# Two pairs of FFN chunks as seven block products each, in a float32 decoder trunk

## The chip, the cores and the metric

One core of a Trainium2 chip runs the whole program. Times are microseconds of device time for one execution; lower is better. The engines are TensorE (PE, with its weight loads as PEld), VectorE (DVE), ScalarE (ACT), GpSimd (POOL) and SyncE (SP), which issues the large loads. Each runs its own instructions in program order and waits on semaphores.

## The reference

The input is x, 256 tokens of 1024 float32 values. Two layers follow, each an FFN, a token mixer and a second FFN, with a norm ahead of each:

```
def rms_norm(x, g):
    y = xf * lax.rsqrt(jnp.mean(xf * xf, axis=-1, keepdims=True) + EPS)
    return y * g
def swiglu(h, w_in, w_out):
    a, b = jnp.split(h @ w_in, 2, axis=-1)
    return (jax.nn.silu(a) * b) @ w_out
...
x = x + 0.5 * swiglu(rms_norm(x, norm_g[l, 0]), ffn_w_in[l, 0], ffn_w_out[l, 0])
x = x + mixer(rms_norm(x, norm_g[l, 1]))
x = x + 0.5 * swiglu(rms_norm(x, norm_g[l, 2]), ffn_w_in[l, 1], ffn_w_out[l, 1])
```

w_in is 1024 x 5632 (2816 columns of a, 2816 of b), w_out is 2816 x 1024. The mixer of layer 0 is a sparse attention over compressed, selected and window keys (NSA), that of layer 1 an attention with forget gates (Fox) on keys and values projected once (KV). The order of stages is FFN 0, NSA, FFN 1, KV, FFN 2, Fox, FFN 3.

## The kernel before

**Numbers in two parts.** A float32 product is made of three matmuls of rounded parts: hi x hi, hi x lo and lo x hi (`three`). hi is a cast to float32r, lo is what the cast leaves. So each weight value is cast on ScalarE and subtracted on VectorE before TensorE uses it.

**Units.** Weights come in units of 128 x 2048 values (1 MB in two transfers). SyncE loads unit u into `raw`, ScalarE casts it to `whi` (`hi`), VectorE writes `wlo` (`lo`), TensorE uses it in 24 matmuls of 128 x 512 (two token tiles x four row blocks x three). Each of the three buffers has three places, and unit u takes place u % 3: the load of u waits for the split of u - 3, the cast of u for TensorE's use of u - 3 (`s_used`).

**An FFN.** The 2816 hidden columns are 11 chunks of 256 (j = 0 to 10). A chunk has two input units a and b, the upper and the lower half of the 1024 rows, each with 256 columns of a and 256 of b; their product stands in the banks `inb[0]` and `inb[1]`, one per token tile. ScalarE takes silu of the a columns (`silu_tile`), VectorE multiplies (`hidden_tile`), four transposes turn the result into `tb[0]` (`hidden_turn`), ScalarE and VectorE split it into `ghi` and `glo`. The chunk's output unit o is 256 rows of w_out; it adds into the four banks `acc`. TensorE's order is a1 b1 o0, a2 b2 o1, and so on: a chunk's output is multiplied one chunk later. Chunks 1 to 9 run in loops (`Fori`) on every engine; the last chunk takes one token tile after the other, so that its hidden part is ready in time. Then the next stage's first unit begins.

**Other work.** GpSimd makes the table of relative biases in FFN 0, adds attention results in NSA, and makes the decay terms at the start of FFN 2. The reciprocal roots of the norm, `rstd`, are applied per token after the matmuls, so TensorE can start before they are known.

Lines: `three` is L403 to L405, turns L512 and L397, `hi` L922 and L935 (loop), `lo` L1312 and L1329 (loop), silu L988, hidden product L1376, its split L997 and L1385, decay terms L1877 to L1881, the adds of the residual L1426 and L1436.

Of the kernel before, what the change touches and what calls it, by code (L numbers as in the profile page):

```python
# [70 lines left out]

TURNS = ["ffn0", "nsa", "ffn1", "kv", "ffn2", "fox", "ffn3"]
# [29 lines left out]
def yoco_trunk(nc, x, norm_g, ffn_w_in, ffn_w_out, nsa_w_in, nsa_cmp_pos, nsa_cmp_w1, nsa_cmp_w2,  # L102
               nsa_w_out, rel_bias, kv_norm_g, fox_w_kvf, fox_b_f, fox_w_q, fox_w_out, final_g, out):
    ctx = ExitStack()
    with ctx:
# [27 lines left out]
        fhi = sb("fhi", [P, 16, GN], F32R)  # L133
        flo = sb("flo", [P, 16, GN], F32R)
# [51 lines left out]
        win_hi = fhi[:, :, :].rearrange("p t n -> p (t n)")  # L186
        win_lo = flo[:, :, :].rearrange("p t n -> p (t n)")
# [3 lines left out]
        ghi_last = fhi[:, :, :].rearrange("p t n -> p (t n)")[:, 0:2 * SEQ].rearrange("p (k n) -> p k n", k=2)  # L191
        glo_last = flo[:, :, :].rearrange("p t n -> p (t n)")[:, 0:2 * SEQ].rearrange("p (k n) -> p k n", k=2)
        gwhi = ghi[:, :, :].rearrange("p a n -> p (a n)")
        gwlo = glo[:, :, :].rearrange("p a n -> p (a n)")
# [4 lines left out]
        finalb = work[:, 0:D]  # L199
# [36 lines left out]
        s_silu = sem("silu_done")  # L236
        s_g = sem("hidden_ready")
# [74 lines left out]
        def _(sp):  # L312
            def load(u, halves, number=None):


                if number is not None or u >= RING:
                    sp.wait_ge(s_lo, (u if number is None else number) - RING + 1)
                for dst, src in halves:
                    sp.dma_start(dst, src).then_inc(s_raw[u % RING], 16)

            def ffn_in(f, j, half, u):
                w = ffn_w_in[f // 2, f % 2][half * 512:(half + 1) * 512, :]
                w = w.rearrange("(k p) n -> p k n", p=P)
                r = raw[u % RING][:, :].rearrange("p (k n) -> p k n", k=4)
                return [(r[:, :, 0:FC], w[:, :, bass.ds(j * FC, FC)]),
                        (r[:, :, FC:2 * FC], w[:, :, bass.ds(j * FC + DFF, FC)])]

            def ffn_out(f, j, u):
                w = ffn_w_out[f // 2, f % 2]
                r = raw[u % RING][:, :].rearrange("p (k n) -> p k n", k=2)  # L330
                return [(r[:, k, :], w[bass.ds(j * FC + k * P, P), :]) for k in range(2)]

            def ffn(f):
                b = U_FFN[f]
                for i in range(2):
                    if f or i:
                        load(b + i, ffn_in(f, 0, i, b + i))
                        continue
                    (ra, wa), (rb, wb) = ffn_in(0, 0, 0, 0)
                    for k, arrived in ((0, s_first), (2, s_raw[0])):  # L340
                        for r, w in ((ra, wa), (rb, wb)):
                            sp.dma_start(r[:, k:k + 2], w[:, k:k + 2]).then_inc(arrived, 16)
                    sp.dma_start(xs[:, 1, :], x[0, P:2 * P, :]).then_inc(s_x[1], 16)
                with sp.Fori(1, NJ) as j:
                    for i in range(3):
                        u = b + 2 + i
                        halves = ffn_in(f, j, i, u) if i < 2 else ffn_out(f, j - 1, u)

                        load(u, halves, 3 * (j - 1) + max(u, RING))
                u = b + FFN_UNITS - 1  # L350
                load(u, ffn_out(f, NJ - 1, u))

            def matrix(w, b, chunks):

                for c, col in enumerate(chunks):
                    for i in range(2):
                        u = b + 2 * c + i
                        wr = w[i * 512:(i + 1) * 512, col:col + CW].rearrange("(k p) n -> p k n", p=P)
                        r = raw[u % RING][:, :].rearrange("p (k n) -> p k n", k=4)
                        load(u, [(r[:, 0:2], wr[:, 0:2]), (r[:, 2:4], wr[:, 2:4])])  # L360
# [4 lines left out]
            for xk in range(2):  # L365
                for i in range(2):
                    u = U_CMP[xk] + i
                    wr = nsa_cmp_w1[0, xk, i * 1024:(i + 1) * 1024, :].rearrange("(k p) n -> p k n", p=P)
                    r = raw[u % RING][:, :].rearrange("p (k n) -> p k n", k=8)
# [18 lines left out]
        def _(pe):  # L388
# [94 lines left out]
            def out_part(slot, t, k, first=False):  # L483

                for n in range(2):
                    mm = out_columns(slot, t, k, n, first=first)
                return mm

            def out_columns(slot, t, k, n, last=False, first=False):
                h_hi, h_lo = (ghi_last, glo_last) if last else (ghi, glo)  # L490
                tok = slice(t * P, (t + 1) * P)
                col = slice(k * D + n * CW, k * D + (n + 1) * CW)
                return three(acc[2 * t + n][:, :], h_hi[:, k, tok], h_lo[:, k, tok],
                             whi[slot][:, col], wlo[slot][:, col], first and k == 0, last and k == 1)

            def out_last(slot, t):

                for n in range(2):
                    out_columns(slot, t, 0, n, True)
                    mm = out_columns(slot, t, 1, n, True)  # L500
                    mm.then_inc(s_used if (t, n) == (1, 1) else s_out_bank, 1)
# [6 lines left out]
            def hidden_turn(need, tiles=range(NT)):  # L508
                pe.wait_ge(s_g, need)
                for k in range(2):  # L510
                    for t in tiles:
# [3 lines left out]

            def ffn(f, following=None):

                b, n0, h0 = U_FFN[f], NJ * f, (NJ + 1) * f
# [5 lines left out]

                unit_in((b + 2) % RING, 0, inb, b + 3)
                hidden_turn(2 * (n0 + 1))
                unit_in((b + 3) % RING, 1, inb, b + 4)
                pe.wait_ge(s_lo, b + 5)
                pe.wait_ge(s_glo, 1 + h0)
                slot = (b + 4) % RING  # L530
                out_part(slot, 0, 0, True)
                out_part(slot, 0, 1)
                out_part(slot, 1, 0, True)
                hidden_turn(2 * (n0 + 2))
                out_part(slot, 1, 1).then_inc(s_used, 1)

                with pe.Fori(2, NJ - 1) as j:
                    for half in range(2):
                        u = b + 2 + half
                        unit_in(u % RING, half, inb, 3 * (j - 1) + u + 1)  # L540
                    pe.wait_ge(s_lo, 3 * (j - 1) + b + 5)
                    pe.wait_ge(s_glo, j + h0)
                    slot = (b + 4) % RING
                    out_part(slot, 0, 0)
                    out_part(slot, 0, 1)
                    out_part(slot, 1, 0)
                    hidden_turn(2 * j + 2 * n0 + 2)
                    out_part(slot, 1, 1).then_inc(s_used, 1)

                u = b + 3 * (NJ - 1) - 1  # L550
                for t in range(NT):
                    for half in range(2):
                        pe.wait_ge(s_lo, u + half + 1)
# [1351 lines left out]
```

## Time and profile before

| | us |
|---|---|
| median of 3 runs | 1053.43 (1053.39 to 1054.06) |
| profiled execution | 1053.35 |
| its span, first to last instruction | 1051.4 |
| TensorE busy | 1040.1 (99%) |
| VectorE busy | 598.2 (57%) |
| ScalarE busy | 525.5 (50%) |
| GpSimd busy | 73.4 (7%) |
| mean granted TensorE clock | 0.995 of full speed |

The profile is of one execution. A span leaves out about 2 us that the measured time has. Start times are microseconds from the first instruction. Matmul records overlap: the distance from start to start, not the duration, is what one costs. The four FFN stages lie at about 0 to 192, 356 to 550, 602 to 788 and 856 to 1046 us.

### The profile page before, as it was taken

The page shows a single profiled execution, that of the slowest core. Times are in us where ns is not written, and L with a number is a line of the kernel's source. Part 1 is how long each engine was busy: PE and PEld are TensorE (multiplying, and loading weights), DVE is VectorE, ACT ScalarE, POOL GpSimd, SP SyncE. Part 2 cuts the span into 40 slices and gives each one's busy share as a digit, 9 for nine tenths or more (in the row PEclk, how much of TensorE's full clock was granted, in tenths as well). Part 3 has the DMA queues.
Part 4 walks back from the last instruction along what each step waited for, and adds up shares of the span by engine and source line. Part 5 has one row for each costly group of instructions (what it writes and reads, how often), then busy time and mean ns, then how long its engine had stood idle before and what let it go on. Part 6 is the DMA issues. An engine that isn't in the chain of part 4 may idle for free.

```text
span 1051.4 us, 14153 instructions
## 1 busy us (share of the span) xinstructions
PE 1040.1 (99%) x5156; PEld 865.4 (82%) x5156; DVE 598.2 (57%) x833; ACT 525.5 (50%) x692; POOL 73.4 (7%) x108
## 2 busy tenths in 40 slices
PE   9999999999999999999999999999999999999997
PEld 7888888888888888888888888888888888888886
DVE  5554454677576564455467765544566656445544
ACT  7434434657475554434456554344356655443443
POOL 0041000000013000000000291000000000000000
PEclk9999999999899999999999999999999999999999
DMA  7686757457401366555545665555446146655541
GB/s 243 239 214 208 218 187 249 145 175 225 136 2 41 120 202 198 191 168 199 183 150 188 221 204 193 184 198 190 170 160 200 42 140 201 199 183 177 199 160 41
DMA packets 128709, 182.45 MB, mean 174 GB/s; under 512 B 5960, under 2 KB 100272, under 8 KB 128544
## 3 DMA queue, kind: packets, MB, share of 16 engines
q1 hardware_dynamic: 127040, 176.18, 50.5%
q0 software_dynamic: 1456, 5.72, 2.4%
q8 instruction: 24, 0.39, 0.2%
q14 instruction: 13, 0.11, 0.0%
q10 hardware_dynamic: 176, 0.05, 0.0%
HBM read 180.34 MB, written 1.59 MB: 173 GB/s over the span
## 4 chain that ended last, share of the span: by engine, by line
PE 97%; DVE 2%; ACT 1%; issue 0%; POOL 0%; POOLq 0%; DVEq 0%; ACTq 0%
PE inb L403 16%; PE inb L405 16%; PE inb L404 16%; PE acc L403 13%; PE acc L405 13%; PE acc L404 13%; PE acc L613 2%; PE tb L512 2%; PE tb L625 2%; PE inb L640 2%; PE inb L637 1%; PE tb L592 1%; PE tb L397 1%; PE acc L397 0%; DVE tlo L1346 0%; PE inb L824 0%
## 5 line engine op out<-in xcount | busy, mean ns | idle before, releaser
L1329 DVE TENSOR_TENSOR wlo<-raw,whi 128x2048 fp32r<-128x2048 f32 x108 | 250.0, 2315 | 233.6 <-ACT whi L935 233.6
L935 ACT CAST whi<-raw 128x2048 fp32r<-128x2048 f32 x108 | 206.5, 1912 | 217.5 <-PE acc L405 117.8
L403 PE MATMUL inb<-whi,thi 128*128 128x512 f32 x720 | 281.7, 391 | 0.0
L405 PE MATMUL inb<-whi,tlo 128*128 128x512 f32 x720 | 280.5, 390 | 0.0
L404 PE MATMUL inb<-wlo,thi 128*128 128x512 f32 x720 | 280.2, 389 | 0.0
L405 PEld LDWEIGHTS inb<-whi,tlo 128*128 128x128 f32 x720 | 135.1, 188 | 28.4
L404 PEld LDWEIGHTS inb<-wlo,thi 128*128 128x128 f32 x720 | 135.2, 188 | 28.0
L403 PEld LDWEIGHTS inb<-whi,thi 128*128 128x128 f32 x720 | 135.2, 188 | 28.0
L1312 DVE TENSOR_TENSOR wlo<-raw,whi 128x2048 fp32r<-128x2048 f32 x55 | 129.1, 2352 | 43.8 <-ACT whi L922 43.5
L403 PE MATMUL acc<-whi,ghi 128*128 128x512 f32 x320 | 128.5, 402 | 0.0
L405 PE MATMUL acc<-whi,glo 128*128 128x512 f32 x320 | 125.1, 391 | 0.0
L404 PE MATMUL acc<-wlo,ghi 128*128 128x512 f32 x320 | 124.6, 389 | 0.0
L922 ACT CAST whi<-raw 128x2048 fp32r<-128x2048 f32 x55 | 105.2, 1918 | 11.7 <-PE acc L405 9.5
L988 ACT ACTIVATE sa<-inb,rstd 128x256 f32<-128x256 f32 x80 | 34.0, 471 | 137.8 <-PE inb L405 137.8
L403 PE MATMUL acc<-whi,thi 128*128 128x512 f32 x224 | 89.4, 399 | 1.3 <-DVE tlo L1346 0.6
L405 PE MATMUL acc<-whi,tlo 128*128 128x512 f32 x224 | 87.6, 391 | 0.0
L404 PE MATMUL acc<-wlo,thi 128*128 128x512 f32 x224 | 87.3, 390 | 0.0
L405 PEld LDWEIGHTS acc<-whi,glo 128*128 128x128 f32 x320 | 60.0, 188 | 12.9
L1376 DVE SCALAR_TENSOR_TENSOR gg<-inb,rstd,sa 128x256 f32<-128x256 f32 x80 | 35.4, 479 | 61.6 <-ACT sa L988 61.6
L404 PEld LDWEIGHTS acc<-wlo,ghi 128*128 128x128 f32 x320 | 60.3, 188 | 11.1
L403 PEld LDWEIGHTS acc<-whi,ghi 128*128 128x128 f32 x320 | 60.1, 188 | 11.0
L403 PEld LDWEIGHTS acc<-whi,thi 128*128 128x128 f32 x224 | 42.1, 188 | 11.5 <-issue 1.2
(231 smaller groups left out, 980.1 us busy)
## 6 DMA issues: line engine op xcount, KB each, us to landing
raw<-in_ffn_w_in SPq DMA_DIRECT2D x174, 512.0 KB, 4.7
raw<-in_ffn_w_out SPq DMA_DIRECT2D x88, 512.0 KB, 4.0
raw<-in_nsa_w_in SPq DMA_DIRECT2D x20, 512.0 KB, 4.1
raw<-in_fox_w_kvf SPq DMA_DIRECT2D x16, 512.0 KB, 4.3
raw<-in_nsa_cmp_w SPq DMA_DIRECT2D x8, 512.0 KB, 4.8
raw<-in_nsa_w_out SPq DMA_DIRECT2D x8, 512.0 KB, 4.5
raw<-in_fox_w_q SPq DMA_DIRECT2D x8, 512.0 KB, 4.5
raw<-in_fox_w_out SPq DMA_DIRECT2D x8, 512.0 KB, 4.6
```

The costliest lines, as they stand in the source:

```text
L403: pe.matmul(o, lh, rh, start=start, stop=False, skip_group_check=True)
L404: pe.matmul(o, lh, rl, start=False, stop=False, skip_group_check=True)
L405: return pe.matmul(o, ll, rh, start=False, stop=stop, skip_group_check=True)
L512: mm = pe.transpose(tb[0][:, k * SEQ + t * P:k * SEQ + (t + 1) * P], gg[:, t, k * P:(k + 1) * P], ident[:, :])
L613: mm = pe.matmul(acc[2 * (n % 2) + h][:, c0:c0 + keys], qT[rows, p, t * P:(t + 1) * P], kT[rows, kidx, 0:keys], start=True, stop=True)
L625: mm = pe.transpose(tb[h][:, i * P:(i + 1) * P], probs[:, n % 2, c:c + P], ident[:, :])
L922: act.copy(whi[u % RING][:, :], raw[u % RING][:, :]).then_inc(s_hi, 1)
L935: act.copy(whi[u % RING][:, :], raw[u % RING][:, :]).then_inc(s_hi, 1)
L988: act.activation(sa[:, t, :], banks[t][:, 0:FC], ACT.Silu, scale=rstd[:, t:t + 1]).then_inc(s_silu, 1)
L1312: dve.tensor_tensor(wlo[u % RING][:, :], raw[u % RING][:, :], whi[u % RING][:, :].bitcast(F32), ALU.subtract).then_inc(s_lo, 1)
L1329: dve.tensor_tensor(wlo[u % RING][:, :], raw[u % RING][:, :], whi[u % RING][:, :].bitcast(F32), ALU.subtract).then_inc(s_lo, 1)
L1376: dve.scalar_tensor_tensor(out=gg[:, t, :], in0=banks[t][:, FC:2 * FC], scalar=rstd[:, t:t + 1], in1=sa[:, t, :], op0=ALU.mult, op1=ALU.mu ...
```

## The change

Chunks 3 and 4, and 7 and 8, become a pair. `KINDS = "nnnsnnsnn"` lists the segments of an FFN: n a single chunk, s a pair. For a pair the input side is the product of the tokens (256 x 1024, four blocks A11 to A22 of 128 x 512) with weights (1024 rows x 512 columns of a and 512 of b, four blocks B11 to B22 of 512 x 512). It is made from seven block products in place of eight, each 12 matmuls:

- on the tokens: S1 = A21 + A22, S3 = A11 - A21, S2 = S1 - A11, S4 = A12 - S2, made by GpSimd once per FFN, then split by ScalarE and VectorE;
- on the weights: T1 = B12 - B11, T3 = B22 - B12, T2 = B11 + T3, T4 = B21 - T2 (as the code forms them), by VectorE once per pair;
- products M1 (A11, B11), M5 (S1, T1), M2 (A12, B21), M6 (S2, T2), M3 (S4, B22), M7 (S3, T3), M4 (A22, T4), combined by VectorE and ScalarE into the four results u3, c12, c22, c21. M2 adds to M1's bank, M3 to M5's, M7 to M6's.

The four weight blocks of a pair are loaded into `nat`, `xn` and `work`, outside the three load buffers, one behind each of four unit loads. A pair's TensorE order is M1 M5 o M2 M6 (o) M3 M7 M4, the first turn, then the next chunk's a, in which the second turn follows. M4 goes into `tb[1]`. The token sums need the tokens times `rstd` in a row layout: two matmuls (`rstd_rows`) turn `rstd` into rows. GpSimd's bias and decay work waits for later units. All loops over chunks are written out, and the last chunk is treated as the others, with two output units at the end. `qT` now lies in `nat`, the final gain in `vx`.

```
+KINDS = "nnnsnnsnn"
+LOADS_AT_ONCE = 1
...
+def ffn_order():
+    order = []
+    for kind, j, rows in SEGMENTS:
+        if kind == "n":
+            order += [("a", j), ("b", j)] + [("o", r) for r in rows]
+        else:
+            order += [("M1", j), ("M5", j), ("o", rows[0]), ("M2", j), ("M6", j)]
+            order += [("o", r) for r in rows[1:]] + [("M3", j), ("M7", j), ("M4", j)]
+    return order + [("o", r) for r in LAST_ROWS]
...
+            def pair_weights(f, n, i):                       # SyncE
+                b, j = U_FFN[f], PAIRS[n]
...
+                elif i == 0:
+                    u = b + UNIT_OF["M7", PAIRS[n - 1]]
+                    sp.wait_ge(s_tw, 4 * (len(PAIRS) * f + n))
+                    sp.wait_ge(s_lo, u + 1)
...
+                    if n < len(PAIRS) and (kind, j) == (("o", 0) if n == 0 else ("b", PAIRS[n - 1] + 2)):
+                        i = 0
+                    if i is not None and kind in "abo":
+                        for i in range(i, i + LOADS_AT_ONCE):
+                            pair_weights(f, n, i)
...
+            def ffn_pair(f, j, rows):                        # TensorE
+                n = len(PAIRS) * f + PAIRS.index(j) + 1
+                product(f, j, "M1", "A11", inb[1], True, False)
...
+                product(f, j, "M5", "S1", tb[1], True, False)
+                out_rows(f, rows[0])
+                pe.wait_ge(s_m1, n)
+                product(f, j, "M2", "A12", inb[1], False, True)
+                product(f, j, "M6", "S2", inb[0], True, False)
+                for r in rows[1:]:
+                    out_rows(f, r)
+                pe.wait_ge(s_m5, n)
+                product(f, j, "M3", "S4", tb[1], False, True)
+                pe.wait_ge(s_u2, n)
+                product(f, j, "M7", "S3", inb[0], False, True)
+                pe.wait_ge(s_c12, n)
+                product(f, j, "M4", "A22", tb[1], True, True)
+                pair_turn(f, j, 0)
...
+            def ffn_chunk(f, j, rows):                       # ScalarE
+                if kind == "s":
+                    pair_hidden_hi(f, before, 1)
...
+                if SEGMENTS[i + 1:i + 2] and SEGMENTS[i + 1][1] == PAIRS[0]:
+                    for name in SPLITS:
+                        tokens_hi(f, name)
+                hi(a + 3)
...
+            def ffn_chunk(f, j, rows):                       # VectorE
+                if pair == PAIRS[0]:
+                    for name in SPLITS:
+                        tokens_lo(f, name)
+                if pair:
+                    t1_weights(f, pair)
+                lo(a + 3)
...
+                for t in range(NT):
+                    hidden_tile(2 * (NSEG * f + i) + t, t)
+                if pair:
+                    t3_weights(f, pair)
+                lo(a + 4)
+                for r in rows:
+                    u = b + UNIT_OF["o", r]
+                    chunk_hidden_lo(f, j)
+                    if u + 3 < b + FFN_UNITS:
+                        lo(u + 3)
+                if pair:
+                    t2_weights(f, pair)
+            def ffn_pair(f, j, rows):                        # VectorE
+                lo(m["M1"] + 3)
+                t4_weights(f, j)
+                lo(m["M5"] + 3)
+                lo(m["M5"] + 4)
+                lo(m["M2"] + 3)
...
+                dve.tensor_tensor(c12, inb[0][:, :], u3, ALU.add).then_inc(s_u2, 1)
+                lo(m["M6"] + 3)
+                for r in rows[1:]:
+                    lo(m["M6"] + 4)
...
+                dve.tensor_tensor(c12, tb[1][:, :], c12, ALU.add).then_inc(s_c12, 1)
...
+                dve.tensor_tensor(c12, c12, sa_p, ALU.mult).then_inc(s_g, 1)
+                lo(m["M3"] + 3)
...
+                dve.tensor_tensor(u3, inb[0][:, :], u3, ALU.add).then_inc(s_u3, 1)
...
+                dve.tensor_tensor(c22, c22, u3, ALU.add).then_inc(s_c22, 1)
+                lo(m["M7"] + 3)
+                pair_hidden_lo(f, j, 0)
...
+                dve.tensor_tensor(c22, c22, sa_p, ALU.mult).then_inc(s_g, 1)
+                lo(m["M4"] + 3)
...
+            def token_sums(f):                               # GpSimd
+                pool.wait_ge(s_lo, U_FFN[f] + 2)
...
+                pool.wait_ge(s_rc, f + 1)
...
+                pool.tensor_tensor(four(c22), a21, a22, ALU.add).then_inc(s_as, 1)
+                pool.tensor_tensor(a21, a11, a21, ALU.subtract).then_inc(s_as, 1)
+                pool.tensor_tensor(a11, four(c22), a11, ALU.subtract).then_inc(s_as, 1)
+                pool.tensor_tensor(a12, a12, a11, ALU.subtract).then_inc(s_as, 1)
...
+            token_sums(2)
+            pool.wait_ge(s_used, U_FFN[2] + UNIT_OF["b", PAIRS[-1] + 2] + 1)
```

## Rows read from the trace of the kernel before

**Rows 1.** The page: busy time of the engines, and the chain that ended last.

```profile
PE 1040.1 (99%) x5156; PEld 865.4 (82%) x5156; DVE 598.2 (57%) x833; ACT 525.5 (50%) x692; POOL 73.4 (7%) x108
...
PE 97%; DVE 2%; ACT 1%; issue 0%; POOL 0%; POOLq 0%; DVEq 0%; ACTq 0%
```

**Rows 2.** Windows, FFN 1: busy us (instructions) by engine, clock, DMA share, GB/s.

```profile
356.00:550.00 194.00, 194.00 (x894) 160.71 (x893) 104.16 (x99) 91.32 (x103) 0.00 (x0) 1.00 0.55 180
```

**Rows 3.** Timeline, TensorE, FFN 1: start, us, engine, line, operation.

```profile
405.39 0.39 PE L403 MATMUL inb<-whi,thi 128*128 128x512 f32 x1
...
410.84 0.39 PE L403 MATMUL inb<-whi,thi 128*128 128x512 f32 x1
```

**Rows 4.** Timeline, ScalarE, FFN 1, one chunk; idle time before in brackets.

```profile
399.69 0.84 ACT L988 ACTIVATE sa<-inb,rstd 128x256 f32<-128x256 f32 x2 [3.53 <-PE inb L405]
...
405.59 1.91 ACT L935 CAST whi<-raw 128x2048 fp32r<-128x2048 f32 x1 [3.26 <-PE acc L405]
...
416.48 0.84 ACT L988 ACTIVATE sa<-inb,rstd 128x256 f32<-128x256 f32 x2 [3.53 <-PE inb L405]
```

**Rows 5.** Groups of instructions, whole span: count, busy us, mean ns, idle before.

```profile
L1385 DVE TENSOR_TENSOR glo<-tb,ghi 128x512 fp32r<-128x512 f32 x40 | 27.3, 683 | 0.0
...
L997 ACT CAST ghi<-tb 128x512 fp32r<-128x512 f32 x40 | 23.2, 579 | 6.0 <-PE tb L512 6.0
```

**Rows 6.** Timeline, FFN 1: two casts and two splits back to back.

```profile
371.89 3.71 ACT L922 CAST whi<-raw 128x2048 fp32r<-128x2048 f32 x2
...
373.82 4.50 DVE L1312 TENSOR_TENSOR wlo<-raw,whi 128x2048 fp32r<-128x2048 f32 x2 [1.31 <-ACT whi L922]
```

**Rows 7.** Chain in order of time, KV stage: broadcast of the roots.

```profile
558.31 0.54 PE acc L859 x4
```

**Rows 8.** Groups of instructions: VectorE's product of two operands from SBUF.

```profile
L1777 DVE TENSOR_TENSOR xn<-xs,work 128x1024 f32<-128x1024 f32 x2 | 2.4, 1220 | 0.0
```

**Rows 9.** Chain in order of time, start of FFN 2.

```profile
598.54 3.04 DVE wlo L1312
...
601.72 0.47 PE acc L403
```

**Rows 10.** Waits, whole span: who waited for whom, us, times, longest.

```profile
PE acc L403 <- DVE wlo L1312: 0.6, 1, 0.6
```

**Rows 11.** Timeline, GpSimd: one add in NSA, and some of the 16 of FFN 2.

```profile
306.13 1.28 POOL L1856 TENSOR_TENSOR xn<-xn,low 128x512 f32<-128x512 f32 x1 [135.65 <-DVE low L1660]
...
598.14 1.28 POOL L1877 TENSOR_TENSOR low<-bias,cmask 128x512 f32<-128x512 f32 x1 [9.83 <-DMA bias<-neg_c_dram]
...
605.65 3.34 POOL L1877 TENSOR_TENSOR low<-bias,cmask 128x512 f32<-128x512 f32 x1
...
619.64 3.94 POOL L1879 TENSOR_TENSOR bias<-bias,cq 128x1024 f32<-128x1024 f32 x1
...
629.33 1.89 POOL L1879 TENSOR_TENSOR bias<-bias,cq 128x1024 f32<-128x1024 f32 x1
631.30 3.23 POOL L1881 TENSOR_TENSOR bias<-bias,cmask 128x512 f32<-128x512 f32 x1
```

**Rows 12.** Timeline, VectorE, beside them.

```profile
629.42 3.94 DVE L1329 TENSOR_TENSOR wlo<-raw,whi 128x2048 fp32r<-128x2048 f32 x1 [2.33 <-ACT whi L935]
```

**Rows 13.** Timeline, FFN 1: first hidden cast, first and third split after it.

```profile
377.40 0.59 ACT L997 CAST ghi<-tb 128x512 fp32r<-128x512 f32 x1 [1.81 <-PE tb L512]
...
379.83 2.29 DVE L1329 TENSOR_TENSOR wlo<-raw,whi 128x2048 fp32r<-128x2048 f32 x1 [0.92 <-ACT whi L935]
...
390.74 2.29 DVE L1329 TENSOR_TENSOR wlo<-raw,whi 128x2048 fp32r<-128x2048 f32 x1 [2.90 <-ACT whi L935]
```

**Rows 14.** Windows, FFN 1, two units' loads in flight; last columns DMA share, GB/s.

```profile
380.00:382.00 2.00, 2.00 (x11) 1.65 (x9) 2.00 (x1) 0.00 (x0) 0.00 (x0) 1.00 1.10 371
```

**Rows 15.** Windows with TensorE under 8 of 8 us; third from last the clock.

```profile
280.00:288.00 8.00, 7.17 (x46) 6.21 (x47) 2.40 (x13) 2.45 (x6) 0.00 (x0) 0.73 0.00 1
...
800.00:808.00 8.00, 7.40 (x46) 6.17 (x45) 5.78 (x22) 5.00 (x9) 0.00 (x0) 1.00 0.79 266
```

More of the change, by code:

```diff
@@ L67, with ring_loads @@
 U_FFN = [U_FFN0, U_FFN1, U_FFN2, U_FFN3]
+def ring_loads():
+    count, last, loads = [0] * RING, [None] * RING, {}
+    for u in range(U_END):
+        if not any(b <= u < b + FFN_UNITS and ORDER[u - b][0] not in "abo" for b in U_FFN):
+            slot = len(loads) % RING
+            count[slot] += 1
+            loads[u] = (slot, count[slot], last[slot])
+            last[slot] = u
+    return loads
+LOADS = ring_loads()
+SPLITS = ["S1", "S2", "S4", "S3"]
 TURNS = ["ffn0", "nsa", "ffn1", "kv", "ffn2", "fox", "ffn3"]
@@ L481, in last_chunk, with rstd_rows @@
                         mm.then_inc(s_tile0, 1)
[L483 to L490, printed above, removed]
+            def rstd_rows(name):
+                pe.wait_ge(s_rstd, NORMS.index(name) + 1)
+                for t in range(NT):
+                    mm = pe.matmul(tb[1][:, t * P:(t + 1) * P], rstd[:, t:t + 1].broadcast_to([P, P]),
+                                   ident[:, :], start=True, stop=True)
+                mm.then_inc(s_rrow, 1)
@@ L500, in out_last, with product @@
-                    mm = out_columns(slot, t, 1, n, True)
+                    out_columns(u, j, t, n, 0)
+                    mm = out_columns(u, j, t, n, 1, last=True)
                     mm.then_inc(s_used if (t, n) == (1, 1) else s_out_bank, 1)
+            def product(f, j, name, a, bank, start, stop):
+                u = U_FFN[f] + UNIT_OF[name, j]
+                a_hi, a_lo = token_block(a)
+                pe.wait_ge(s_lo, u + 1)
+                for k in range(4):
+                    col = slice(k * CW, (k + 1) * CW)
+                    mm = three(bank[:, :], a_hi[:, k], a_lo[:, k], whi[u % RING][:, col], wlo[u % RING][:, col],
+                               start and k == 0, stop and k == 3)
+                mm.then_inc(s_used, 1)
@@ L574, in ffn @@
-                out_last((u + 3) % RING, 1)
+                for n in range(2):
+                    mm = out_columns(u, j, 1, n, 1)
+                mm.then_inc(s_used, 1)
+                out_last(u + 1, last, 1)
             def tail(cols):
@@ L1395, in ffn @@
             def ffn(f):
-                b, n0, h0 = U_FFN[f], NJ * f, (NJ + 1) * f
-                hidden(2 * n0, acc)
+                b = U_FFN[f]
+                for t in range(NT):
+                    hidden_tile(2 * NSEG * f + t, t, acc)
                 if f:
```

536 lines of the change are left out of this document (374 added, 162 removed).

## The prediction, made before the result was known

> **What bounds the kernel now.** I read the page from the top: busy shares, then the chain that ended last. TensorE is busy 1040.1 of 1051.4 us, and 97% of the chain is its own work [rows 1]. So time can only be won by giving it fewer matmuls, and each new wait of TensorE counts in full. The stage windows say the same of the FFN stages: in 356 to 550 us TensorE has no idle time while VectorE works 104 of 194 us [rows 2].
>
> Next, the pace. From the start of one 24-matmul unit to the next, 405.39 to 410.84, is 5.45 us, so a 128x512 matmul costs 0.227 us (its record's 0.39 us overlaps the next one's) [rows 3]. Silu to silu is 16.79 us for a chunk: 3 x 5.45, and 0.44 for the four transposes [rows 4].
>
> Beside it, in one chunk VectorE does three splits of 2.29 us, two hidden products and a 0.68 us split; ScalarE three casts of 1.91 us and smaller work [rows 4, 5]. Their idle time ends with TensorE's units, not the reverse. Back to back, two splits take 4.50 us, a pace of 2.21, and two casts 3.71, a pace of 1.80 [rows 6].
>
> **What is removed.** A pair of chunks needs 2 x 2 x 24 = 96 matmuls for its input side; seven products of 12 are 84. 12 x 0.227 = 2.72 us go per pair, 21.8 us over eight pairs. Output rows and transposes keep their number (8 per pair before and after).
>
> **What is added on TensorE.** Two broadcast matmuls per FFN for the row of reciprocal roots. The nearest row is the KV stage's two, four pieces in 0.54 us [rows 7]: four FFNs make 2.2 us; bounds 1.1 (one piece each) and 4.4 (twice the row: its result has 16 partitions, the new one 128). Left: 19.6 us.
>
> **What is added on VectorE, and what of it shows.** Each product is its own unit and needs a whole cast and a whole split of 128x2048, but feeds TensorE for only 12 x 0.227 = 2.72 us in place of 5.45. On top come four combinations of weight blocks per pair (t1 to t4), the same shape and kind as a split, so 2.21 us each; the nearest other row, 128x1024 from two SBUF operands in 1.22, doubles to 2.44, the upper end [rows 8]. Also per pair: adds and products of 128x512 at 0.68 (pace 0.6), and casts of 0.58 on ScalarE [rows 5].
>
> I lay one pair out, t = 0 being the start of M1, each engine in program order, a cast starting 0.2 us after the TensorE unit that frees its buffer (405.39 to 405.59) [rows 3, 4], a dependent operation 0.1 after its releaser. The cast of unit o waits for the turn in front of M1, so the split of o starts at 2.65. From there VectorE does not rest: t2 4.86, split M2 7.07, t4 9.28, split M6 11.49 to 13.8. TensorE: M1 0, M5 2.7, o 5.4, M2 10.9, ready for M6 at 13.6, starts 13.9: late by 0.3. In the first pair split M3 ends 16.0, split M7 18.6, u2 19.2, split M4 21.4, add for C12 22.1, its product 22.8, split a5 25.0, u3 25.6. TensorE: M3 16.6, M7 19.35, M4 22.15, turn 24.9, then a5 can start only at 25.7, since u3 still reads its bank: late 0.4. The second turn, after a5, waits for silu, product and combination at 31.3 against 31.15: 0.15. So u2 and the C12 add also arrive within 0.1 of the need. A real stop costs about 0.24 more, as a matmul after one takes 0.47 until the next in place of 0.23 [rows 3, 9]; where VectorE is the limit this is absorbed. I take 1.4 us for a first pair. The second pair has two output rows (o5, o6), so M3 and later have 5.45 us more air: M6 0.3 + 0.24, a9 0.15, second turn 0.1: 0.8. Together 2.2 us per FFN, 8.8 in all. Bounds: nothing stops (0); or each late step, the near misses too, stops for itself and pays the 0.24: 0.95 + 5 x 0.24 = 2.15 in a first pair, 0.55 + 3 x 0.24 = 1.27 in a second, 13.7 in all.
>
> **GpSimd's token sums.** Per FFN: two adds and two multiplications of 128x1024, four combinations of 128x512. Rows: 512 with two full operands 1.28, so 2.5 for 1024 (the broadcast 1024 took 1.89); collisions with VectorE stretch 512 to 3.34 and 1024 to 3.94, about 2.05 for each split met, and a split at 629.42 took 3.94 in place of 2.29 beside a GpSimd operation that ended at 631.2 [rows 11, 12]. In FFN 1 the first turn ends at 377.2 (its cast starts at 377.40) [rows 13]. The broadcasts and two short casts put the row of roots at 378.4, and b1, o0 and a turn put chunk 2 at 377.2 + 0.54 + 2 x 5.45 + 0.44 = 389.1. From 378.4 the sums take 2 x 2.5 + 4 x 1.28 = 10.1 us and 2.2 for each split met, two or three of those from 379.83 to 390.74 [rows 13]: end at 393 to 395. The split of o1 then takes VectorE to 395.3, four token blocks (2.4) to 397.7, 8.6 us into the chunk, and t1 starts. Behind it lie split M1, two hidden products (0.9), t3 and split M5, 4 x 2.21 + 0.9 = 9.7 us, and M5 is wanted at 16.8 + 2.7 = 19.5: late only when t1 starts after 9.8. So zero, with 1.2 us of air. If every one of the six meets a split, 2 x 3.94 + 4 x 3.34 = 21.2 us, t1 starts at 12.3, and 3.0 us per FFN are lost.
>
> The Trainium skill (SBUF — State Buffer, "SBUF: two separate sides") has the pair of ports shared by VectorE and GpSimd as an exclusive lock for the whole instruction, which VectorE wants when both inputs lie in SBUF. The 3.94 us split agrees: it ended 2.14 after GpSimd's operation. By the rule each engine simply takes turns, which is the 10.1 + 2.2 per split above; by sharing of bandwidth both would run slower together, with about the same end.
>
> **Moved work, at nothing.** SyncE: the bytes stay equal, 4 MB per pair now come between the loads of the two chunks before, about 2.1 MB per 5.45 us for four units, 385 GB/s. The row at full share has 371 GB/s [rows 14], so loads fall about 1 us behind, while a load issued three loads ahead has some 11 us. For the second pair, its first block waits for the split of M7, and the output rows of chunk 3 queue behind it: issued at 18.6, 2 MB at that rate with some 3 us of latency, there by 27, wanted at 30.5. If that cover is gone, each us late counts. GpSimd: bias loads move later in FFN 0, but end before its end, wanted only in the NSA stage. The decay work, 598.14 to 634.5 [rows 11], leaves the start of FFN 2 for its last six units (34 us); at the start TensorE waited 0.6 us for a split of 3.04 us [rows 9, 10], and I put the same, 0.8 with the restart, at the Fox boundary, net 0 (bounds -0.8 and 0.8).
>
> **Sum.** Against the profiled execution (1053.35, span 1051.4, median of the runs 1053.43): 1053.35 - 21.8 + 2.2 + 8.8 = 1042.6. The air of 1.2 us at t1 and 0.3 us at most others is thin, and later delays pass on one for one in a VectorE chain without rest; I add 0.3 us per pair, 2.4 in all, from the upper end of t1 to t4 (4 x 0.23 = 0.9 us per pair, of which half the chain has cover). Forecast 1045.0.
>
> **Rivals.**
> - *Nothing shows.* The splits are a little ahead of my table and all new waits find their semaphores up: 1053.4 - 19.6 = 1033.8. For it: most lateness is 0.1 to 0.4 us. Against: in the first pair VectorE's sum from 2.65 to 25.6 leaves no gap. 10%.
> - *Near misses stop.* Stalls of 13.7 us and the 2.4 of the sum: 1053.35 - 19.6 + 16.1 = 1049.9, and to no change with a little more. For it: three steps of a first pair arrive within 0.15 us. 17%.
> - *Token sums late, slower.* GpSimd loses its turn to a split at each of six operations. t1 lies in front of the split of M1 in VectorE's queue and all later splits behind it; from a start after 12.1 us into chunk 2 (2.3 us lost) what is left of the gain is gone. At the bound: 1045.0 + 4 x 3.0 = 1057. For it: in 605 to 635 five of thirteen operations took over 3.2 us. Against: there are only three or four splits in the window, not six. 18%.
> - *TensorE's clock falls.* Short stops are new. In 280 to 288 TensorE was busy 7.17 of 8 us at a granted 0.73; but 800 to 808 (7.40) kept 1.00 [rows 15]. If each of eight pairs lost what that stretch did (0.27 x 8 = 2.2 us): 1062. 4%. The Trainium skill (TensorE: Matmul & The Clock Gate, "A second HAM failure mode") warns of micro-idles between groups of matmuls; the 280 us row could be that, the other row speaks against it.
>
> **Numbers.** Forecast with 1041 to 1049: 51%. No change for this kernel means within 0.2%, 2.1 us. Faster: 51 + 10 + most of the near misses (9) = 70; same 9 (the rest of them and some late sums); slower 21. The range leaves out the far end of "nothing shows" and of the clock: 1036 to 1059.
>
> **What would show it.** Right: 96 fewer 128x512 matmuls; waits of TensorE for VectorE, 0.3 to 0.5 us each, at M6, at the unit behind a pair and at the second turn, 2 to 3 us per FFN; VectorE busy from the split of o to u3; granted clock 1.00. Wrong: ScalarE waiting for GpSimd at the token blocks by more than 1 us, M1 or M5 waiting, casts that wait for DMA, or TensorE stops of over 1 us.

## The result, and the profile after

The changed kernel takes 1043.77 us (median; 1042.84 to 1044.41), the kernel before 1053.74 beside it: a ratio of 0.9903 (95% interval 0.9888 to 0.9917). It is faster by 10 us. 1045.0 was forecast, with 1041 to 1049. (One of the four executions of the kernel before took 5969.89 us; without it their median is 1053.43.)

The profiled execution took 1042.84 us, with a span of 1041.1 and a mean granted clock of 0.997. First the page of the kernel after, its busy times and its chain, and then its stage window of 356 to 550 us (PE, PEld, DVE, ACT and POOL busy with counts, granted clock, DMA share, GB/s). They answer to [rows 1, 2].

```profile
PE 1028.7 (99%) x5076; PEld 847.2 (81%) x5076; DVE 765.6 (74%) x925; ACT 587.4 (56%) x732; POOL 151.6 (15%) x140
PE 92%; DVE 4%; issue 2%; ACT 1%; DMA 0%; ACTq 0%; DVEq 0%
```

```profile
356.00:550.00 194.00, 193.84 (x879) 158.16 (x878) 148.01 (x127) 109.43 (x114) 18.78 (x8) 1.00 0.54 184
```

TensorE still has no gap that counts, but VectorE works 148 us of this window where it worked 104 [rows 2], and 4% of the chain of waits are its own where 2% were [rows 1]. TensorE's instructions fall from 5156 to 5076: 96 matmuls less, and four short pieces more in each FFN for the row of roots. That is how a kernel looks that has bought matmuls with another engine's time. At each boundary between stages the tokens `xs` are turned in two groups of eight. Stage by stage, from the second group ahead of a stage to the first group behind it (for FFN 3, to the end):

| us | before | after | difference |
|---|---|---|---|
| FFN 0 | 181.5 | 179.3 | -2.2 |
| NSA | 155.85 | 154.84 | -1.0 |
| FFN 1 | 179.02 | 176.83 | -2.2 |
| KV | 44.70 | 44.70 | 0 |
| FFN 2 | 179.82 | 176.82 | -3.0 |
| Fox | 68.09 | 68.02 | -0.1 |
| FFN 3 | 189.2 | 187.0 | -2.2 |

(Left out are the six stretches between two such groups, 6.3 to 7.8 us each and equal in both within 0.04, and the start of the kernel, which became 0.3 longer.) An FFN has 24 matmuls fewer, 5.4 us, and keeps 2.2 of them, 3.0 in FFN 2. NSA's 1.0 comes from no edit: its length went from 154.8 to 157.0 over the kernels below, by the clock granted in 264 to 304 us. In the profiled executions it was 0.96 there after, and 0.91 before and in two more kernels below (hidden tiles moved by 448 bytes, and both edits). So where two totals differ by 1 or 2 us, the FFN stages are read beside them. The first window row is of the kernel after, the second of the kernel before:

```profile
264.00:304.00 40.00, 38.80 (x293) 33.29 (x291) 26.26 (x118) 25.23 (x62) 0.92 (x1) 0.96 0.21 69
```

```profile
264.00:304.00 40.00, 38.95 (x280) 34.02 (x278) 26.07 (x111) 23.22 (x56) 0.00 (x0) 0.91 0.25 80
```

Now one pair, the first of FFN 1, in the timeline of TensorE after (start, duration, line, operation). Each row is the first matmul of a unit or product, and the distance to the next is what the unit cost.

```profile
403.11 0.48 PE L571 MATMUL inb<-whi,thi 128*128 128x512 f32 x1
...
417.07 0.47 PE L571 MATMUL inb<-whi,bhi 128*128 128x512 f32 x1
...
422.74 0.47 PE L571 MATMUL inb<-whi,bhi 128*128 128x512 f32 x1
...
425.54 0.45 PE L571 MATMUL tb<-whi,thi 128*128 128x512 f32 x1
...
428.35 0.60 PE L715 MATMUL tb<-ident,gg 128*128 128x128 f32 x4
...
429.11 0.47 PE L571 MATMUL inb<-whi,thi 128*128 128x512 f32 x1 [0.16 <-DVE work L1751]
...
440.64 0.40 PE L571 MATMUL acc<-whi,fhi 128*128 128x512 f32 x1
...
446.24 0.60 PE L706 MATMUL tb<-ident,gg 128*128 128x128 f32 x4
```

M1 starts at 403.11, M6 at 417.07, M7 at 422.74, M4 at 425.54, the turn at 428.35, the next chunk's a at 429.11. Behind a turn, as at M1, the first matmul takes 0.48 in both kernels and its unit 0.11 us more, without any wait. Elsewhere a first matmul of 0.47 where others take 0.39 came late, if only a little. The trace writes an idle time only at the last, 0.16 us, so the waits are read off the starts. The last two rows are an output unit: 24 matmuls in 5.60 us, where 5.45 was a unit in [rows 3].

### The profile page after: what moved, and what is told of

Read it like the earlier page. It is cut to its first block, busy times and chain, and to the rows that moved or that the text cites. A ratio compares the mean times of both kernels' runs of the same rounds, so it can differ in the third digit from the quotient of the medians.

```text
span 1041.1 us, 13003 instructions
## 1 busy us (share of the span) xinstructions
PE 1028.7 (99%) x5076; PEld 847.2 (81%) x5076; DVE 765.6 (74%) x925; ACT 587.4 (56%) x732; POOL 151.6 (15%) x140
## 4 chain that ended last, share of the span: by engine, by line
PE 92%; DVE 4%; issue 2%; ACT 1%; DMA 0%; ACTq 0%; DVEq 0%
PE acc L571 13%; PE acc L573 13%; PE acc L572 13%; PE inb L571 12%; PE inb L573 12%; PE inb L572 12%; PE acc L837 2%; PE inb L864 2%; PE tb L849 2%; PE tb L572 1%; PE tb L573 1%; PE tb L571 1%; PE tb L706 1%; DVE wlo L1586 1%; PE inb L861 1%
## 5 line engine op out<-in xcount | busy, mean ns | idle before, releaser
L1154 ACT CAST whi<-raw 128x2048 fp32r<-128x2048 f32 x131 | 250.5, 1915 | 52.3 <-PE inb L573 19.9
L571 PE MATMUL inb<-whi,thi 128*128 128x512 f32 x528 | 210.1, 398 | 0.6 <-DVE work L1751 0.6
L573 PE MATMUL inb<-whi,tlo 128*128 128x512 f32 x528 | 206.2, 391 | 0.0
L572 PE MATMUL inb<-wlo,thi 128*128 128x512 f32 x528 | 205.9, 390 | 0.0
L571 PE MATMUL acc<-whi,fhi 128*128 128x512 f32 (+1 forms) x384 | 149.0, 388 | 0.0
L573 PE MATMUL acc<-whi,flo 128*128 128x512 f32 (+1 forms) x384 | 148.3, 386 | 0.0
L572 PE MATMUL acc<-wlo,fhi 128*128 128x512 f32 (+1 forms) x384 | 148.2, 386 | 0.0
L573 PEld LDWEIGHTS acc<-whi,flo 128*128 128x128 f32 (+1 forms) x384 | 70.5, 184 | 15.9
L572 PEld LDWEIGHTS acc<-wlo,fhi 128*128 128x128 f32 (+1 forms) x384 | 70.5, 184 | 15.4
L571 PEld LDWEIGHTS acc<-whi,fhi 128*128 128x128 f32 (+1 forms) x384 | 70.5, 184 | 15.3
```

What stands on the lines that cost most here:

```text
L571: pe.matmul(o, lh, rh, start=start, stop=False, skip_group_check=True)
L572: pe.matmul(o, lh, rl, start=False, stop=False, skip_group_check=True)
L573: return pe.matmul(o, ll, rh, start=False, stop=stop, skip_group_check=True)
L1154: act.copy(whi[u % RING][:, :], unit_source(u)).then_inc(s_hi, 1)
```

## The experiments

Open were: why output units had become slower, what sets the 0.9 us of stops in a first pair, whether VectorE's new sums cost anything, how much air the token sums have, whether the second pair pays, and whether what was found adds up.

**The hidden tiles moved by 64 bytes.** Before, the hidden splits of chunks 0 to 9 lay in `ghi` and `glo`. Only the last chunk used `fhi`, which lies behind `vx` (8256 bytes of a partition, so no multiple of 256). After, all chunks use `fhi` and `flo`. (The second pad keeps every tile behind them where it was, against multiples of 128.)

```
         work = sb("work", [P, 3072])
+        pad = sb("pad", [P, 16])
         fhi = sb("fhi", [P, 1024], F32R)
         flo = sb("flo", [P, 1024], F32R)
+        pad2 = sb("pad2", [P, 16])
```

> Changed kernel with 64 bytes of padding in front of the two split hidden tiles (fhi, flo) and 64 behind, so that their start in a partition falls on a multiple of 128 bytes and every other tile keeps its offset from such a multiple. Theory (where the stationary operand starts in SBUF sets the pace): output units go from 5.60 to 5.45 us, 44 of them, 6.6 us less, 1037.3 from 1043.8; input units stay at 5.45 to 5.56. Rival (the pace of 0.233 comes from the waits ahead of the unit or from written-out code): no change, 1043.8.

Measured: 1043.27 us (1043.21 to 1043.33), ratio 0.9899 (0.9884 to 0.9914). No change; an output unit takes 5.58 to 5.59. Lying off a multiple of 128 bytes is not what slows it.

**All tiles behind `vx` moved by 64 bytes.**

```
         vx = sb("vx", [P, NT * H // 2 * VP])
+        pad = sb("pad", [P, 16])
```

> Changed kernel with 64 bytes of padding behind vx, so that bias, work, the split hidden tiles, low, gate weights and the identity all start on multiples of 128 bytes. Theory: as the run with the hidden tiles alone, 1037.3, and up to 3 us less still where work, gate weights and the identity are read by TensorE (attention in NSA and Fox, turns). Rival: no change, 1043.8.

Measured: 1043.83 us, ratio 0.9902 (0.9887 to 0.9917). No change either: output units keep 5.59, and moving the other tiles behind `vx` by 64 bytes gains nothing.

**The kernel before, with its hidden tiles moved.** Its loops stay.

```
         tlo = sb("tlo", [P, KT, SEQ], F32R)
+        pad = sb("pad", [P, 16])
         ghi = sb("ghi", [P, 2, SEQ], F32R)
         glo = sb("glo", [P, 2, SEQ], F32R)
+        pad2 = sb("pad2", [P, 16])
```

> Kernel before, loops and all, with the two split hidden tiles (ghi, glo) moved by 64 bytes and nothing else moved against multiples of 128. Theory: the output units of chunks 0 to 9, 10 per FFN, go from 5.45 to 5.60 us, 40 x 0.155 = 6.2 us more, 1059.9 from 1053.7. Rival (written-out code or waits): no change, 1053.7.

Measured: 1058.59 us (1057.37 to 1059.77), ratio 1.0041 (1.0027 to 1.0056): 4.7 us slower. The timeline of TensorE in this kernel has 18 output matmuls and the turn behind them:

```profile
402.02 0.40 PE L405 MATMUL acc<-whi,ghi 128*128 128x512 f32 x1
...
406.22 0.60 PE L514 MATMUL tb<-ident,gg 128*128 128x128 f32 x4
```

4.20 us for 18, or 0.2333 each. In the kernel before the same 18 take 4.08, 0.227 each:

```profile
399.49 0.39 PE L403 MATMUL acc<-whi,ghi 128*128 128x512 f32 x1
...
403.57 0.60 PE L512 MATMUL tb<-ident,gg 128*128 128x128 f32 x4
```

The loops are unchanged, so the address alone makes the slower pace. FFN 1 takes 180.40 us, 1.4 more.

**The hidden tiles moved by 192 and by 448 bytes.** The edit of the first experiment with `[P, 48]` and `[P, 112]` ahead of `fhi`.

> Changed kernel, split hidden tiles moved up by 192 bytes: start 128 bytes over a multiple of 256, 384 over one of 512 (thi, tlo, whi, wlo and the token blocks, all read at 0.227 us, start 128 over a multiple of 256 and of 512; the runs at 192, at 0 over 256 were read at 0.233). Theory A (128 over a multiple of 256 is what is fast): output units 5.45 us, 6.6 us less, 1037.2. Theory B (it has to be the offset in 512 of the moving operand): 5.60, 1043.8, no change.

> Changed kernel, split hidden tiles moved up by 448 bytes: start 128 bytes over a multiple of 512, as thi and whi. Theories A and B of the run at 192 both expect output units of 5.45 us and 1037.2. Rival (where these tiles lie does not matter at these distances; the pace comes from the order of the code): 5.60, 1043.8.

Measured: 1039.08 us (1038.13 to 1039.75), ratio 0.9864 (0.9848 to 0.9881), and 1038.54 (1038.07 to 1039.76), ratio 0.9861 (0.9845 to 0.9878). An output unit in the timeline of the first:

```profile
440.35 0.39 PE L573 MATMUL acc<-whi,fhi 128*128 128x512 f32 x1
...
445.80 0.38 PE L708 MATMUL tb<-ident,gg 128*128 128x128 f32 x2
```

5.45 us: the old pace is back, and with it some 5 us. FFN 1 takes 175.40 us with 448 bytes, 1.43 less than after. The ten units that had become slower give 1.5 and the last one 0.15; a little comes back as stops, since TensorE now asks for M6 earlier. The four FFN stages together are 5.8 shorter in the profiled execution, and NSA 1.4 longer (156.21, at 0.91).

**All tiles moved by 128 bytes**, so that `whi` changes its place in 256 bytes, but not its distance to `thi` and `fhi`.

```
+        pad = sb("pad", [P, 32])
         raw = [sb(f"raw{s}", [P, UNIT]) for s in range(RING)]
```

> Changed kernel with 128 bytes of padding ahead of the first tile, so that every tile moves by 128: whi, wlo, thi, tlo and the token blocks now start on multiples of 256, the split hidden tiles 64 over one. Theory A (the stationary operand must start 128 over a multiple of 256): all 128x512 matmuls at 0.233, some 3000 more of them than now, 20 us more, 1064. Theory C (stationary and moving operand must have the same offset in 256): input units stay at 0.227, output units at 0.233, 1043.8.

Measured: 1043.24 us (1042.89 to 1043.44), ratio 0.9903 (0.9888 to 0.9918). Input units kept 0.227 us a matmul and output units 0.233. In this run `thi` is as fast at its new place as it was at the old one, and `fhi` as slow, so the place alone doesn't decide. What counts is the distance from the stationary operand (`thi`, `fhi`) to the moving one (`whi`), modulo 256 bytes, worked out from the sizes of the tiles in their order in the kernel:

| kernel, operand | distance mod 256 | us a matmul |
|---|---|---|
| before, `thi` and `ghi`; all tiles moved, `thi` | 0 | 0.227 |
| 192 and 448 bytes, `fhi` | 0 | 0.227 |
| after and all tiles moved, `fhi`; before with hidden tiles moved, `ghi` | 64 | 0.233 |
| hidden tiles, or all tiles behind `vx`, moved by 64 bytes, `fhi` | 128 | 0.233 |

A distance of 192 was not tried, and no run shows why the distance matters.

**The weight sums on one column.** What VectorE's t1 to t4 cost. The kernel leaves out the other 2047 columns of each sum, so its results are wrong, but its order of work is the same.

```
-                dve.tensor_tensor(combined(f), b12, b11, ALU.subtract).then_inc(s_tw, 1)
+                dve.tensor_tensor(combined(f)[:, 0:1], b12[:, 0:1], b11[:, 0:1], ALU.subtract).then_inc(s_tw, 1)
```

(and the other three likewise)

> Changed kernel in which VectorE forms one column of each weight combination t1 to t4 in place of 2048, so the seven products use wrong weights; 32 operations of 2.29 us leave VectorE. Theory (VectorE without rest sets the stops inside a pair): stops of 0.8 us in a first pair and 0.3 in a second fall to 0.3 and 0.1, about 0.7 us per FFN, 2.5 to 3.5 us in all, 1040.8. Rival (the stops are the price of changing banks and of the turn's dependent chain): within 1 us of 1043.8. If VectorE's load were worth what the prediction put on it (11.2 us): 1033.

Measured: 1044.05 us (1043.51 to 1044.94), ratio 0.9907 (0.9892 to 0.9923); FFN 1 is 0.07 shorter, so the theory misses and the rival holds. M6 is no longer late (13.90 us after M1), but M7 then waits longer, and the pair takes 26.00 as before. Taking 9 us per pair from VectorE gives nothing, so from M3 on its sum of work isn't the limit. The chain of waits of the kernel after shows what is (start, length, what):

```profile
417.21 0.02 ACT sa L1277
...
417.80 1.92 ACT whi L1154
...
421.95 0.69 DVE gg L1739
...
424.75 0.70 DVE gg L1745
...
426.08 2.28 DVE wlo L1586
428.36 0.61 DVE work L1751
```

("issue" pieces between these rows are left out.) From the end of M2: silu, cast of M7, its split, u2, split of M4, the adds for C12, the split of a5, u3, and a5. The timelines of VectorE and ScalarE in that kernel have the gap:

```profile
416.84 2.29 DVE L1586 TENSOR_TENSOR wlo<-work,whi 128x2048 fp32r<-128x2048 f32 x1
419.74 2.29 DVE L1586 TENSOR_TENSOR wlo<-nat,whi 128x2048 fp32r<-128x2048 f32 x1 [0.62 <-ACT whi L1154]
```

```profile
417.21 0.69 ACT L1277 ACTIVATE sa<-inb,rstd 128x512 f32<-128x512 f32 x1 [0.79 <-PE inb L573]
417.80 1.91 ACT L1154 CAST whi<-nat 128x2048 fp32r<-128x2048 f32 x1
```

VectorE rests 0.62 us because the cast of M7 stands behind the silu.

**The cast ahead of the silu**, to shorten this chain by the silu.

```
                 hi(m["M5"] + 4)
+                hi(m["M2"] + 3)
                 act.wait_ge(s_used, m["M2"] + 1)
...
                 act.activation(sa_p, inb[1][:, :], ACT.Silu, scale=rstd[:, 0:1]).then_inc(s_silu, 1)
-                hi(m["M2"] + 3)
```

> Changed kernel, with ScalarE's cast for the unit three behind M2 (M7 in a first pair, M3 in a second) in front of the silu, not behind it. Theory (the stop at the end of a pair is a chain from the end of M2: silu, cast M7, split M7, u2, split M4, C12 add, product, split a5, u3, with TensorE waiting at its end): cast M7 starts 0.59 us earlier, the unit behind a first pair 0.5 us earlier, second pairs 0.1: 2 to 2.5 us in all, 1041.5. Rival (VectorE's sum of work from the split of o on sets it): split M3 ends where it ended, under 0.5 us in all, 1043.5.

Measured: 1041.65 us (1041.07 to 1043.4), ratio 0.9893 (0.9877 to 0.9910): 2.1 us better than after by the medians, and 1.8 in the four FFN stages of the profiled executions (FFN 1 takes 176.38). ScalarE and VectorE in its timeline:

```profile
416.96 1.92 ACT L1154 CAST whi<-nat 128x2048 fp32r<-128x2048 f32 x1 [0.84 <-PE inb L573]
418.79 0.68 ACT L1278 ACTIVATE sa<-inb,rstd 128x512 f32<-128x512 f32 x1
...
418.91 2.29 DVE L1586 TENSOR_TENSOR wlo<-nat,whi 128x2048 fp32r<-128x2048 f32 x1
```

The cast starts 0.19 us after the first matmul of M6 in place of 0.73, the split follows the one before without a rest, and the pair takes 25.55 us in place of 26.00. The chain read above is the right one.

**Six more sums on GpSimd, and one more.** The same edit with `range(6)` and `range(1)`.

```
+                for _ in range(6):
+                    step(pool.tensor_tensor(four(c22), a21, a22, ALU.add))
                 pool.tensor_tensor(four(c22), a21, a22, ALU.add).then_inc(s_as, 1)
```

> Changed kernel with six more adds of 128x512 on GpSimd in front of the four token combinations, in each FFN (same result). They take 1.3 us each, 7.9 us; the last combination ends near 397.7 in FFN 1 in place of 389.8, t1 starts about 13.3 us into chunk 2 in place of 8.3. The prediction's working (M5 is late when t1 starts after 9.8): M5 and what follows 3.5 us late, 14 us in all, 1058. Rival (more air than worked out, since ScalarE's casts and the ring hold more): under 7 us, below 1051.

> Changed kernel with one more add of 128x512 on GpSimd in front of the four token combinations, in each FFN (same result). Six took 2.0 us each with the splits that they met; one moves t1 from 8.3 to 9.6 or 10.3 us into chunk 2. Theory (t1 has air until 9.8, and each us behind that is one of TensorE): 0 to 0.5 us per FFN, 1043.8 to 1045.8. Rival (no air): 1.3 to 2.0 us per FFN, 1049 to 1052.

Measured with six: 1074.0 us (1073.38 to 1075.77), ratio 1.0198 (1.0181 to 1.0216), 7.6 us per FFN, twice what was expected. First GpSimd in the timeline of this kernel, then what TensorE waited for, then two windows behind it (columns as above):

```profile
392.29 11.99 POOL L2199 TENSOR_TENSOR work<-kT 128x512 f32<-128x512 f32 x6
```

```profile
PE tb L706 <- DVE gg L1644: 4.7, 1, 4.7
```

```profile
408.00:416.00 8.00, 4.81 (x21) 3.56 (x19) 6.31 (x5) 5.77 (x7) 2.03 (x2) 0.96 0.00 0
416.00:424.00 8.00, 6.44 (x21) 5.30 (x22) 8.00 (x7) 3.64 (x5) 0.00 (x0) 0.61 0.00 0
```

The six adds took 2.0 us each: 1.3 alone, and more where they met a split. The sums end 14.0 us into chunk 2 (it begins at 396.06), t1 starts at 16.16, and M5 is late by 7.15, where the prediction's rule (one for one from 9.8) gives 6.4. But it is late by another way. What is late first is not M5 but the turn of chunk 2: VectorE does the hidden product behind the blocks, t1 and the split of M1, and TensorE stands 4.7 us. The granted clock of the next 8 us is 0.61, a mix of the two levels 2.4 and 1.2 GHz: the last 11 matmuls of M1 took 4.09 us, 1.6 more than at 0.227. The turn 4.9 late, and 2.2 more in the turn and M1, make M5's 7.15.

With one: 1045.34 us (1044.8 to 1046.37), ratio 0.9927 (0.9913 to 0.9941). FFN 1 and 2 stay at 176.82 and 176.83; FFN 0 is 0.9 us longer. So in FFN 1 and 2 the air takes one add. FFN 0 has less, and its timelines of VectorE and TensorE show why:

```profile
50.67 2.29 DVE L1674 TENSOR_TENSOR kT<-nat 128x2048 f32<-128x2048 f32 x1
```

```profile
56.85 0.48 PE L571 MATMUL inb<-whi,thi 128*128 128x512 f32 x1
...
60.50 0.47 PE L571 MATMUL tb<-whi,bhi 128*128 128x512 f32 x1 [0.66 <-DVE wlo L1586]
```

Chunk 2 begins at 39.89 here, so t1 starts 10.78 into it, 0.98 behind the 9.8 of the prediction, and M5 comes 3.65 us after M1 where it comes 2.83 in the kernel after, 0.8 late. In FFN 1 t1 starts at 9.39 and nothing is late. The rule of 9.8, one for one, holds in both FFNs. Without the add t1 starts at 9.46 in FFN 0, since two multiplications (8.14 us) and two combinations (3.21 each) take longer there beside VectorE's splits: the air is 0.3 us in FFN 0, and not 1.2.

**One pair in place of two.**

```
-KINDS = "nnnsnnsnn"
+KINDS = "nnnsnnnnnn"
```

> Changed kernel with only the first of the two pairs per FFN; chunks 7 and 8 are single ones, 36 units per FFN in place of 39. The sum by its terms: a second pair is worth 2.72 us less 0.3 of stops, so 4 x 2.4 = 9.7 us more than the changed kernel, 1053.5. Theory (one pair pays only for its own fixed costs: row of roots, stops, slower output units): the kernel with one pair is level with the kernel before, 1053.7. Rival (the second pair is where the stops are, as its loads come late): under 5 us more, below 1049.

Measured: 1055.13 us (1052.45 to 1055.5), ratio 1.0004 (0.9994 to 1.0014). FFN 1 takes 179.12, where it took 179.02 before and 176.83 after: the second pair is worth 2.3 us per FFN, and one pair alone just pays for the roots, its stops and the slower output units.

**Both edits together.** The edit for 448 bytes and the cast ahead of the silu.

> Changed kernel with both: the split hidden tiles 448 bytes up (128 over a multiple of 512) and ScalarE's cast in front of the silu. Theory (two separate costs, 5.2 and 2.1 us): 1036.5 from 1043.8. Rival (the faster output units give back air that the chain at the end of a pair needs, since TensorE arrives earlier): 1038 or more.

Measured: 1038.86 us (1035.81 to 1039.06), ratio 0.9854 (0.9838 to 0.9871), not told apart from 448 bytes alone; 2 us less had been expected. FFN 1 is 175.20, only 0.2 shorter than 175.40. The timeline of TensorE says why:

```profile
404.12 0.47 PE L573 MATMUL inb<-whi,thi 128*128 128x512 f32 x1
...
418.08 0.47 PE L573 MATMUL inb<-whi,bhi 128*128 128x512 f32 x1
```

M6 starts 13.96 us after M1, as in the kernel after, though the output unit in between is 0.15 shorter: here VectorE's back-to-back splits and sums set M6, and what TensorE wins in front of it is waited away. With 448 bytes alone it is 13.96 too. A first pair takes 25.57 us here, 25.81 with 448 bytes alone and 25.55 with the cast moved alone: once the cast is moved, the faster output unit in front gives the pair nothing. The four FFN stages are together 0.7 us shorter than with 448 bytes alone, where the cast gave 1.8 on the kernel after, and that is hidden by NSA, 157.04 us against 156.21 there and 154.84 after, at 0.91 in the same 40 us as above. Both this kernel and the one with 448 bytes beat before and after.

## Why the prediction was right, and where only its total was

The time, 1043.8, is 1.2 us from the forecast, and the mechanism held: 96 matmuls less, short waits for VectorE beside them, no transfer or engine that took over. But two terms were wrong by some 6 us each, and they cancelled. That is luck: with the stops alone put right, the forecast would have been 1039.3, under its own range.

| term, us in all | predicted | found |
|---|---|---|
| 96 matmuls less | -21.8 | -21.8 |
| rows of roots | +2.2 | +1.8 |
| stops in and behind the pairs, with the margin | +11.2 | +5.5 |
| slower output units | 0 | +6.2 |
| decay terms moved | 0 | -0.8 |
| NSA's clock | 0 | -1.0 |
| sum | -8.4 | -10.1 |

The profiled execution fell by 10.5. The first term is 96 x 0.227; the others are read off starts in FFN 1 and multiplied by four (the last two off the stages), and an error of 0.3 per FFN could hide in them. NSA's 1.0 is a difference of two executions and no property of the change.

*Rows of roots.* In the kernel after, the turn in front of the two broadcasts takes 0.44 us to the next start and they take 0.36. In the kernel before, the same turn leads to b after 0.36 (376.76 to 377.12). So they cost 0.44; 0.54 was taken from [rows 7].

```profile
373.83 0.60 PE L706 MATMUL tb<-ident,gg 128*128 128x128 f32 x4
374.27 0.61 PE L655 MATMUL tb<-ident,rstd 128*128 128x128 f32 x4
374.63 0.48 PE L571 MATMUL inb<-whi,thi 128*128 128x512 f32 x1
```

*M6 late by 0.3.* Its start is right, 13.96 us after M1 where 13.9 was laid out, and so is the split of M6 that ends then. But it is only 0.08 late, for TensorE, with a slower output unit in front, needs 13.88 itself. With the pace restored it does wait, 0.25.

*"VectorE does not rest" to u3.* Wrong from the split of M7 on. The layout let every cast be ready; the cast of M7 was not, for it needs the silu done first, and that needs M2. a5 came at 26.00 us after M1, against 25.7 laid out, so the place of the stop was right, but its cause was a chain over three engines, not VectorE's sum. The weight sums on one column (no gain) and the cast moved ahead (1.8 us in the FFN stages) show it. So of the signs named for a right forecast, the fewer matmuls, the stop behind the pair and the clock came; a wait of 0.3 at M6 and a VectorE without rest did not.

*The size of the stops.* A first pair takes 26.00 us; seven products (19.04), a turn (0.36), an output unit of 5.60 and the 0.11 of M1 behind its turn make 25.11, which leaves 0.89. A second pair leaves 0.39, and the second turns 0.05 each: 1.4 us per FFN where 1.4 + 0.8 was put. Part of the error was the price of a near miss: 0.24 for a stop, from the 0.47 us of a first matmul [rows 3, 9]. That is the length of its record; in the trace of before too, the matmul behind the one at 601.72 starts at 602.02, 0.30 later in place of 0.23. In the kernel after it is 0.31, and the near misses at M6, M7 and M4 of a first pair cost 0.17, 0.22 and 0.09 with it. The margin of 0.3 per pair had nothing to pay for: without t1 to t4, FFN 1 is only 0.07 shorter.

*Slower output units.* Not seen, though it was in the trace of before: the last chunk's matmuls, on `fhi`, 12 of them in 2.80 us, ran at 0.233.

```profile
536.85 0.40 PE L403 MATMUL acc<-whi,fhi 128*128 128x512 f32 x1
...
539.65 0.38 PE L512 MATMUL tb<-ident,gg 128*128 128x128 f32 x2
```

The change moves ten more units per FFN onto that tile, 1.5 us. The diff's renaming of `ghi` to `fhi` was read as of no cost. This is the step that failed, a term put at nothing without a reason, and the stops that were put too high covered it.

*Token sums.* The layout had the sums end at 393 to 395 and t1 start 8.6 us into chunk 2. GpSimd and VectorE of the kernel after:

```profile
375.47 6.87 POOL L2193 TENSOR_TENSOR kT<-kT,work 128x1024 f32<-128x1024 f32 x2 [9.69 <-ACT work L1243]
...
388.48 1.29 POOL L2204 TENSOR_TENSOR kT<-kT 128x512 f32<-128x512 f32 x1
```

```profile
394.46 2.29 DVE L1674 TENSOR_TENSOR kT<-nat 128x2048 f32<-128x2048 f32 x1
```

The sums end at 389.8 in this kernel, whose times lie about 3 us earlier here than those of before, and t1 starts 8.3 us into the chunk (it begins at 386.17). The rival in which they come late needed 9.8, and did not come. The extra adds show that it is real, and that FFN 0 was nearer to it than the layout of FFN 1 said. (The rival's own bound doesn't add up: t1 at 12.3 loses 2.5 by the rule, not 3.0.) What the two engines do to each other stands in three rows between them:

```profile
382.42 1.30 POOL L2198 TENSOR_TENSOR work<-kT 128x512 f32<-128x512 f32 x1
383.13 2.74 DVE L1586 TENSOR_TENSOR wlo<-raw,whi 128x2048 fp32r<-128x2048 f32 x1 [1.21 <-ACT whi L1154]
383.80 3.21 POOL L2200 TENSOR_TENSOR kT<-kT 128x512 f32<-128x512 f32 x1
```

The split ends 2.15 us behind the end of the first add, about its length alone (2.29), and the second add 1.14 behind the end of the split, less than its 1.3: each ran in its turn, and its wait is inside its row. The lock of the Trainium skill (SBUF — State Buffer, "SBUF: two separate sides") agrees with these rows.

*Decay terms.* They were put at net nothing: 0.8 won where FFN 2 starts and 0.8 lost at the Fox boundary. The win came, the loss did not: GpSimd's rows run from 742.12 and end at 774.2, 5.5 us before the second group of turns ahead of Fox (779.69).

```profile
742.12 1.30 POOL L2273 TENSOR_TENSOR low<-bias,cmask 128x512 f32<-128x512 f32 x1 [116.67 <-PE inb L573]
...
772.90 1.30 POOL L2277 TENSOR_TENSOR bias<-bias,cmask 128x512 f32<-128x512 f32 x1
```

*SyncE's loads and the clock.* Right. Casts waited for in-weights by DMA 4.8 us in six times, none over 1.1, for out-weights 1.3 in three, and none was passed on to TensorE; the prediction had named casts that wait for DMA as a sign of being wrong, and these were too short for that. The FFN window kept 1.00.

## What to carry to other kernels

Before a change that gives a matmul operand another tile, work out both operands' addresses: here an offset of 64 bytes cost a third of what the change could have given, and no engine's idle time shows it. When work is traded from the bounding engine to another, lay out the chain over all engines and not the sum of one, since the order of a cast and a silu was worth more here than four sums of 2.2 us each. And check each stage by itself: the layout of FFN 1 gave 1.2 us of air, and FFN 0 had 0.3. And take the price of a wait from the distance between starts, not from a longer record.

## What was not expected of the hardware

- **Operand distance.** A 128x512 float32r matmul cost 0.227 us where stationary and moving tile lay a multiple of 256 bytes apart in the partition, and 0.233 where they were off by 64 or 128. Over the output units of this kernel that is 5 to 6 us of 1044. Why is not shown.
- **A late matmul is cheap.** The record of a first matmul after a short wait is 0.47 long, but the next one starts only 0.08 later than it would have.
- **The clock after a stop.** Stops of under 1 us kept a granted 1.00 in FFN 1; a stop of 4.7 us was followed by 8 us at a mean of 0.61.
